# A second weight chunk split one block earlier into a borrowed buffer, and a few scale factors computed later

## The reference

```python
x = x + res_w * (1 + gate) * rms_norm(y, g_post)       # residual of sublayer k - 1
h = rms_norm(x, g_pre) * (1 + scale) + shift           # norm of sublayer k
proj = h @ w                                           # first matrix of sublayer k
```

## Time and profile before

| | us |
|---|---|
| median of 3 runs | 2109.1 |
| lowest and highest run | 2108.68, 2111.03 |
| the profiled execution | 2106.61 |
| its span, first to last instruction | 2104.8 |

### The profile page before, as it was taken

How to read it: one execution, slowest core, us unless ns; L and a number is a source line. 1 busy time by engine, 2 the same in 40 slices (tenths; PEclk the granted TensorE clock), 3 DMA queues, 4 the chain that set the end, 5 groups by cost and what they waited for, 6 DMA issues and landing times.

```text
span 2104.8 us, 25824 instructions
## 1 busy us (share of the span) xinstructions
PE 1967.4 (93%) x9588; PEld 1437.4 (68%) x9588; DVE 1378.6 (65%) x2203; ACT 847.8 (40%) x1127; POOL 62.5 (3%) x95
## 2 busy tenths in 40 slices
PE   3899999998999999999999999998899989889998
PEld 2788777776888788778777888776544447764443
DVE  6889776767888788877776888876411146642112
ACT  3344554665443543454655534564200035421000
POOL 0000000000000000000000000021000001000000
PEclk9999999999999999999999999999899999989999
DMA  9999553435897789744444799763799996359997
GB/s 395 376 377 371 182 187 146 170 125 221 338 364 315 287 344 376 292 173 159 173 144 152 295 371 378 209 238 130 283 421 421 421 356 242 123 216 421 421 421 329
DMA packets 98192, 597.88 MB, mean 284 GB/s; under 512 B 20256, under 2 KB 23712, under 8 KB 27424
## 3 DMA queue, kind: packets, MB, share of 16 engines
q1 hardware_dynamic: 91616, 585.18, 71.1%
q10 hardware_dynamic: 6464, 11.15, 1.6%
HBM read 595.21 MB, written 1.09 MB: 283 GB/s over the span
## 4 chain that ended last, share of the span: by engine, by line
PE 72%; DVE 12%; DMA 7%; ACT 5%; issue 3%; POOL 1%; SPq 0%; DVEq 0%; ACTq 0%
PE gu L2718 11%; PE acc L2328 10%; PE acc L2332 10%; PE acc L2331 10%; PE tr L2718 7%; PE gu L2328 5%; DMA proj<-ada_stream 5%; PE gu L2332 5%; PE gu L2331 5%; DVE w_lo L1367 3%; PE acc L2718 3%; PE tr L2468 3%; ACT w_hi L701 2%; DVE tf L2182 2%; DVE proj L1432 2%
## 5 line engine op out<-in xcount | busy, mean ns | idle before, releaser
L1367 DVE TENSOR_TENSOR w_lo<-stage,w_hi 128x2048 fp32r<-128x2048 f32 x231 | 527.6, 2288 | 87.8 <-ACT w_hi L701 87.4
L701 ACT ACTIVATE w_hi<-stage 128x2048 fp32r<-128x2048 f32 x232 | 442.5, 1912 | 211.6 <-PE acc L2332 203.2
L1432 DVE SCALAR_TENSOR_TENSOR proj<-proj,c_row 128x1024 f32<-128x1024 f32 x240 | 291.6, 1218 | 51.3 <-DMA proj<-ada_stream 40.3
L2328 PE MATMUL acc<-w_hi,hT_hi 128*128 128x512 f32 x672 | 277.4, 413 | 6.8 <-DVE z_mix L2077 2.8
L2332 PE MATMUL acc<-w_hi,hT_lo 128*128 128x512 f32 x672 | 264.7, 394 | 0.0
L2331 PE MATMUL acc<-w_lo,hT_hi 128*128 128x512 f32 x672 | 264.2, 393 | 0.0
L2328 PE MATMUL gu<-w_hi,hT_hi 128*128 128x512 f32 x640 | 254.2, 397 | 8.3 <-DVE pair L1504 7.1
L2332 PE MATMUL gu<-w_hi,hT_lo 128*128 128x512 f32 x640 | 250.4, 391 | 0.0
L2331 PE MATMUL gu<-w_lo,hT_hi 128*128 128x512 f32 x640 | 250.0, 391 | 0.0
L2328 PE MATMUL acc<-w_hi,yT_hi 128*128 128x512 f32 (+1 forms) x460 | 180.8, 393 | 2.8 <-ACT proj L1147 2.7
L2332 PE MATMUL acc<-w_hi,yT_lo 128*128 128x512 f32 (+1 forms) x460 | 178.8, 389 | 0.0
(11 more groups left out here) (270 smaller groups left out, 2525.9 us busy)
## 6 DMA issues: line engine op xcount, KB each, us to landing
stage<-wstream SPq DMA_DIRECT2D x312, 1024.0 KB, 5.8
proj<-ada_stream SPq DMA_DIRECT2D x120, 1024.0 KB, 7.6
w_raw<-wstream SPq DMA_DIRECT2D x72, 1024.0 KB, 18.9
z_mix<-wstream SPq DMA_DIRECT2D x12, 1024.0 KB, 16.5
more_yT<-wstream SPq DMA_DIRECT2D x12, 1024.0 KB, 17.7
more_prob<-wstream SPq DMA_DIRECT2D x12, 1024.0 KB, 16.8
more_proj<-wstream SPq DMA_DIRECT2D x12, 1024.0 KB, 18.1
tok<-gate_rows SPq DMA_DIRECT2D x10, 512.0 KB, 4.3
```

The costliest lines, as they stand in the source:

```text
L701: act.activation(w_hi[:, n % PARTS, :], stage[:, n % STAGES, :], ACT.Copy).then_inc(hi_ready, 1)
L1367: dve.tensor_tensor(w_lo[:, n % PARTS, :], stage[:, n % STAGES, :], w_hi[:, n % PARTS, :].bitcast(F32), ALU.subtract).then_inc(chunk_ready, 1)
L1432: ins = dve.scalar_tensor_tensor(w, w, 1.0, c_row[:], ALU.mult, ALU.mult, accum_out=dst)
L2328: ins = pe.matmul(dst, l_hi, r_hi, start=start, stop=False, skip_group_check=True)
```

## The change

- Two tiles `spare_hi` and `spare_lo` (128 x 2048 each) are laid over the start of `qk`. For the sublayers k = 1 to 6 chunk n + 1 is split there, whole, by new helpers `hi_spare` (ACT) and `lo_spare` (DVE), before the old sublayer ends.
- At the end of a feed-forward, `hi_spare` stands behind `hi` of the last down chunk on ACT, and `lo_spare` stands ahead of `lo` of that chunk on DVE. In `out`, both stand behind the fourth chunk's split and ahead of `ahead`.
- `ahead(n)` then counts `hi_ready` and `chunk_ready` by two, for n and n + 1.
- The halves within the norm stay for k = 8 alone, and so does DVE's wait for the root.
- `first_columns` reads chunk n + 1 from the spare tiles.
- `factors(k + 1)` stands behind the first residual instead of ahead of it, for all sublayers but the last.

```diff
+        spare_hi = nc.alloc_sbuf_tensor_at("spare_hi", [P, CW], F32R, offset=qk_at)
+        spare_lo = nc.alloc_sbuf_tensor_at("spare_lo", [P, CW], F32R, offset=qk_at + CW * 4)
+        spare_chunks = [b["n"] + 1 for step, b in plan if step[0] == "norm" and 1 <= step[1] <= 3 * DEPTH]
 ACT
+            def hi_spare(n):
+                act.wait_ge(landed[slots[n][0]], 16 * (slots[n][1] + 1))
+                act.activation(spare_hi[:], stage[:, n % STAGES, :], ACT.Copy).then_inc(spare_high, 1)
             def ahead(n):
-                if n < n_chunks:
+                if n + 1 in spare_chunks:
+                    act.wait_ge(landed[slots[n][0]], 16 * (slots[n][1] + 1))
+                    act.wait_ge(pe_used, n + 1)
+                    act.activation(w_hi[:, n % PARTS, :], stage[:, n % STAGES, :], ACT.Copy).then_inc(hi_ready, 2)
+                elif n < n_chunks:
                     hi(n)
...
                 hi(n0 + 3 * nb - 1)
+                hi_spare(n0 + 3 * nb + 1)
                 silu(nb - 1)
...
-                        hi_half(b["n"] + 1, 0)
+                        if k > 3 * DEPTH:
+                            hi_half(b["n"] + 1, 0)
                         by_root(b, k, 0)
...
-                        hi_half(b["n"] + 1, 1)
+                        if k > 3 * DEPTH:
+                            hi_half(b["n"] + 1, 1)
...
                         hi(b["n"] + c)
+                    hi_spare(b["n"] + 5)
                     ahead(b["n"] + 4)
 DVE
+            def lo_spare(n):
+                dve.wait_ge(spare_high, spare_chunks.index(n) + 1)
+                dve.tensor_tensor(spare_lo[:], stage[:, n % STAGES, :], spare_hi[:].bitcast(F32), ALU.subtract)
             def ahead(n):
-                if n < n_chunks:
+                if n + 1 in spare_chunks:
+                    dve.wait_ge(hi_ready, n + 1)
+                    dve.tensor_tensor(w_lo[:, n % PARTS, :], stage[:, n % STAGES, :], w_hi[:, n % PARTS, :].bitcast(F32),
+                                      ALU.subtract).then_inc(chunk_ready, 2)
+                elif n < n_chunks:
                     lo(n)
...
                     block_(2 + peeled, i)
+                lo_spare(n0 + 3 * nb + 1)
                 lo(n0 + 3 * nb - 1)
                 silu(nb - 1)
...
-                    if k and chunks and k < 3 * DEPTH + 2:
-                        lo_half(b["n"] + 1, 0, split_norms.index(k) + 1)
                     scaled(0)
...
                         scaled(1)
-                        dve.wait_ge(rs_done, norm_request(b, k, 1))
-                        lo_half(b["n"] + 1, 1, 0)
+                        if k > 3 * DEPTH:
+                            dve.wait_ge(rs_done, norm_request(b, k, 1))
+                            lo_half(b["n"] + 1, 1, 0)
                         rest(1)
...
+                    residual(k, b, 0)
                     if k < NSUB - 1:
                         factors(k + 1)
-                    residual(k, b, 0)
...
                     lo(b["n"] + 3)
+                    lo_spare(b["n"] + 5)
                     ahead(b["n"] + 4)
 PE, first_columns
+                        high, low = (spare_hi, spare_lo) if n in spare_chunks else (w_hi[:, s, :], w_lo[:, s, :])
```

More of the change, by code:

```diff
@@ L411, in build @@
         hi_ready = sem("hi_ready")
+        spare_high = sem("spare_high")
         pe_used = sem("pe_used")
@@ L2200, in _ @@
                     chunks = k < 3 * DEPTH or (k - 3 * DEPTH) % 2 == 0
-                    if k and chunks and k < 3 * DEPTH + 2:
-                        lo_half(b["n"] + 1, 0, split_norms.index(k) + 1)
                     scaled(0)
                     if k == 3 * DEPTH + 2:
-                        lo_half(b["n"] + 1, 0, split_norms.index(k) + 1)
+                        lo_half(b["n"] + 1, 0, 1)
                     if k == 0 or not chunks:
@@ L2365, in first_columns @@
                             lhs = hT_hi[:, 4 * part + k, t * P:(t + 1) * P]
-                            for w in (w_hi, w_lo):
-                                pe.matmul(dst(t), lhs, w[:, s, k * 512:k * 512 + width], start=r % 2 == 0 and k == 0 and w is w_hi,
+                            for w in (high, low):
+                                pe.matmul(dst(t), lhs, w[:, k * 512:k * 512 + width], start=r % 2 == 0 and k == 0 and w is high,
                                           stop=False, skip_group_check=True)
@@ L2371, in first_columns @@
                             ins = pe.matmul(dst(t), hT_lo[:, 4 * part + k, t * P:(t + 1) * P],
-                                            w_hi[:, s, k * 512:k * 512 + width], start=False, stop=r % 2 == 1 and k == 3,
+                                            high[:, k * 512:k * 512 + width], start=False, stop=r % 2 == 1 and k == 3,
                                             skip_group_check=True)
```

## The result

The changed kernel took 2126.2 us (median of 5 runs, 2120.0 to 2128.7), the kernel before beside it 2109.1: 1.0076 times as long, 95% interval 1.0059 to 1.0093. The direction was forecast; the size was not: 17 us where 8.9 were expected, and outside the range. The profiled execution has a span of 2121.0 us, 16.2 more than before's.

The account below looks back on a forecast made before the run. PE was taken to bound the kernel, without a gap inside feed-forwards, while at borders it waits for a DVE, ACT and POOL chain. 9.82 + 0 - 0.95 = +8.87 us on 2109.1 gave 2118.0 us, 8-in-10 range 2113 to 2122.

Parts of the forecast that it names:

- The stall: Ends of feed-forwards 0, 2, 3, 5: `lo_spare` delays the silu's product, 2.54 us at three, 2.20 at feed-forward 2; 9.82 lost.
- Factors: Factors behind the first residual: 0.61 us gained at borders after feed-forwards, 0.34 into sublayer 8; 0.95 in all, bounds 0.4 to 1.5.
- Norm halves: Six borders lose two DVE and two ACT halves each; nothing gained, upper bound 0.7 us per border.
- `out`: Added splits in `out`, twice: adds still wait for POOL's root, a tie; 0 us, bounds 0 and 0.1 each.
- The rival that they held the border: Norm halves held the border in all six norms: 13.7 us given back, 2104.3; chance 0.05.
- the one that the stall is hidden: Stall at the feed-forward's end is hidden, only the factors remain: 2108.2, or 2113 with half hidden; chance 0.10.
- The sum: Whole kernel: 9.82 + 0 - 0.95 = +8.87 us, median 2118.0, slower by 0.42%.
- from that point to the first matrix of the next sublayer each border takes as long as before: Borders behind the four stalls, from L2468's transposes on: time unchanged, less 0.1 to 0.3 us.
- the first rival: Clock falls in PE's new gaps, up to 1.64 us each: four falls 2124.6, one or two 2119.6 to 2121.3; chance 0.15.
- of that size: Clock rival's evidence: PE gaps in norms 1 and 2 likened to the new 2.5 us gaps; one lost the clock, one did not.

Follow-up runs that it names:

- kernel 8: Changed kernel with nine useless 512-column matmuls on PE in each stall and the gate row's store requested early (sublayers 2, 3, 5): 2116.7 us, ratio 1.0044.
- kernel 7: Changed kernel with `lo_spare` in two halves, behind the silu's product and behind `turn_lo`, and the gate row's store early: 2108.0 us, ratio 1.0000.
- the stall alone: Kernel before with only the added splits at the four feed-forward ends, read by nobody; norm halves and factors as before: 2119.2 us, ratio 1.0054.
- the second trace: Changed kernel run again unchanged, for its mean and another trace: 2121.8 us over 6 runs, ratio 1.0067.
- kernel 3: Changed kernel with nine useless 512-column matmuls on PE in each of the four stalls, store in its late place: 2126.3 us, ratio 1.0083.

## Why the prediction was wrong

*The stall: right.* Forecast 9.82 us in four ends; the product starts 9.74 later after the silu in all (2.55, 2.13, 2.51 and 2.55), and end 2 gave the smaller step for the reason given, DVE was late there already.

*Factors: right.* From product to adds the borders are 0.13, 0.31 and 0.13 shorter at 1, 3 and 4, and 0.05 at 6 (in kernel 8, where no fall lies in that stretch): 0.62 against 0.61. Into sublayer 8 the products start right behind DVE's last split, without the 0.23 us of the earlier trace rows:
```profile
1726.74 1.23 DVE L1406 TENSOR_TENSOR w_lo<-stage,w_hi 128x1024 fp32r<-128x1024 f32 x1 [0.19 <-ACT w_hi L874]
1727.89 1.28 DVE L2182 TENSOR_TENSOR tok<-acc,tok 128x512 f32<-128x512 f32 x2
```

*Norm halves, `out`: right.* From the adds to the last `hT_lo` the four norms take 18.86, 17.78, 17.27 and 17.79 us in kernel 7, which lacks the halves, and 18.85, 17.77, 17.29 and 17.78 in the kernel before. The rival that they held the border is dead, and so is the one that the stall is hidden.

*The sum: right as far as it goes.* 8.87 forecast; 8.1 measured at full clock, 9.0 with PE kept busy (2117.3 against 2108.3, and 2118.0 was the forecast).

*What failed* is the step "from that point to the first matrix of the next sublayer each border takes as long as before", and with it the choice against the first rival. I gave the fall of the clock in the new gaps 0.15 and let the forecast rest on nothing of it, where the runs lost 6.9 us more to the clock than the kernel before. Its time, 2124.6, is what the kernel takes (2123.4), but that it fits so well is partly luck: one fall behind a stall costs 1.28 us at the end of feed-forward 5, not 1.64. In the first trace the clock fell at one stall of the four, in two of the norms behind them, and elsewhere. And the stall alone lost 3.1 us more to the clock than the kernel before, not 6.6. My evidence was thin: two gaps in norms, one with a fall and one without. I read that as odds against it, where one fall out of two would have meant half the price as the likeliest case, 2121.3, and a range up to 2125 or so. Also, neither gap was "of that size". In the kernel before PE stood still for 1.53 us in norm 1 and 1.36 in norm 2:
```profile
243.85 1.12 PE L2344 MATMUL tr<-const,tok 128*128 128x128 f32 x4 [1.53 <-ACT tok L1273]
...
510.57 0.66 PE L2344 MATMUL tr<-const,tok 128*128 128x128 f32 x4 [1.36 <-ACT tok L1273]
```
In the norm PE still has short work around the gap; at the end of a feed-forward it stands still for 2.6 us in one piece, ahead of work that everything waits for. A fall in a norm can cost nothing: in norm 4 kernel 7 has one (894 us) and the kernel before none, at 17.27 against 17.29 us. The Trainium skill (TensorE: Matmul & The Clock Gate, "HAM oscillation — how this bites in real kernels") has it that PE's waits for data put it back to the half clock, so that the next work starts cold, but for waits longer than these stalls. Here the second trace shows as much at four stalls of four, three of them of 2.57 to 2.59 us, and the first at one of four.

*Left open.* Why the changed kernel lost 3.8 us more to the clock than the stall alone. Why the late slices cost 9 us in kernel 3 and next to nothing in the changed kernel. And how the falls outside the borders (29 to 41 us of lost full-speed time in the traces of changed and unchanged kernels) depend on what went before.

## What to carry to other kernels

A stall put into a stretch where TensorE has no gap was paid here in its own length and then partly again in clock: 8 to 9 us of stall brought 7 of lower clock in the changed kernel and 3 with the stall alone, so price the second part unless work fills the gap. Before a helper is put ahead of a step on the chain, look for the idle time behind that step on the same engine: the same subtraction cost nothing in two halves right behind the product. When a test that takes one cost away leaves the time as it was, split each run's time by its granted clock first: here it showed a gain of 7 us and a new loss of 8.

## What the runs showed of the hardware

- The fall at the end of feed-forward 5 held the clock at 0.50 for about 3.4 us, 1.7 us of full speed, of which 1.28 were lost on the border. Falls change their place from trace to trace of the same kernel: behind feed-forward 0 the changed kernel had none in one trace, with a stop of 2.59 us, and lost 3.4 us of full speed in the next, with a stop of 3.41.
- 2.2 us of useless matmuls in a stall of 2.6 kept the clock at 1.00 at three ends of one trace, and over eight runs 6 to 7 us of lost clock away. At the fourth end the stop grew by a late slice to 2.17 us behind the matmuls, and the clock fell.
- At the ends of feed-forwards a 4 KB store of 1024 scattered elements took 12 to 16 us from request to landing. Slices of 1 MB requested just ahead of it were late by up to 7.6 us there; with the store elsewhere, by 1.6 at most in twelve ends.
- A gap put down to a late input can have another floor: ahead of norm 8 PE started work that waited for nothing that the profile shows only after 5.07 us.
